# Mixing attention: two heads a step in the two halves of the TensorE array, and fewer key blocks for the neighbourhood heads

## The reference, cut to what matters

```python
def neighbourhood_attention(q, k, v, kc, vc, rpb):
    ...
    w_start = np.clip(q_col - NA_KW // 2, 0, GRID_W - NA_KW)[..., None]
    valid = (k_col >= w_start) & (k_col < w_start + NA_KW)   # 16 of the 64 columns
    ...
        s_lat = einsum('bjqhd,bijshd->bhjqis', q_r, k_r) * scale + bias
        s_lat = where(valid, s_lat, NEG_INF)
        s_ctx = einsum('bjqhd,blhd->bhjql', q_r, kc) * scale
        p = softmax(concatenate([s_lat, s_ctx], axis=-1))
        return einsum(p_lat, v_r) + einsum(p_ctx, vc)

def window_gqa_attention(q, k, v, kc, vc, sink):
    # 128 queries see keys at most 128 away, the context, and a sink logit
```

## Time and profile before

| | |
|---|---|
| median of 3 runs | 4348.28 us (4348.02 to 4357.41) |
| profiled execution, its own time | 4366.82 us |
| its span | 4365.0 us |
| mean granted clock of TensorE | 0.926 of full speed |
| busy, share of the span | PE 89%, DVE 44%, ACT 28%, POOL 24% |

### The profile page before, as it was taken

How to read it: one execution, slowest core, us unless ns; L and a number is a source line. 1 busy time by engine, 2 the same in 40 slices (tenths; PEclk the granted TensorE clock), 3 DMA queues, 4 the chain that set the end, 5 groups by cost and what they waited for, 6 DMA issues and landing times.

```text
span 4365.0 us, 55857 instructions
## 1 busy us (share of the span) xinstructions
PE 3873.9 (89%) x21157; PEld 3208.4 (74%) x21157; DVE 1926.2 (44%) x2729; ACT 1200.5 (28%) x1742; POOL 1031.9 (24%) x419
## 2 busy tenths in 40 slices
PE   3999996898969999889999688979997899888998
PEld 2888885756748888768888575667886799578755
DVE  7555444155553432444353614653226644530134
ACT  2212121044322121222111212433223523311353
POOL 1332331200112322213332120013442233023301
PEclk9999997988979999989999798989997999788998
DMA  4333321100013322123332121012332122012201
GB/s 163 125 126 125 106 96 57 45 26 5 25 44 96 111 91 92 63 68 105 101 111 92 44 87 37 9 39 72 96 96 87 46 81 87 1 53 66 74 1 49
DMA packets 88275, 316.33 MB, mean 72 GB/s; under 512 B 10688, under 2 KB 11712, under 8 KB 87488
## 3 DMA queue, kind: packets, MB, share of 16 engines
q1 hardware_dynamic: 85056, 300.44, 21.3%
q10 hardware_dynamic: 3072, 13.90, 1.0%
HBM read 312.20 MB, written 2.10 MB: 72 GB/s over the span
## 4 chain that ended last, share of the span: by engine, by line
issue 74%; POOL 16%; PE 8%; POOLq 0%; DVE 0%; ACT 0%; ACTq 0%
POOL w_parts L460 16%; PE psum L1418 4%; PE psum L1736 1%; PE psum L1720 1%; PE psum L1759 1%; PE psum L1745 1%; PE psum L1724 0%; POOLq L459 0%; POOLq L464 0%; PE psum L1738 0%; DVE final L1346 0%; DVE final L1347 0%; DVE sq_sum L1272 0%; POOLq L460 0%; PE psum L1726 0%
## 5 line engine op out<-in xcount | busy, mean ns | idle before, releaser
L1418 PE MATMUL psum<-h_parts,w_parts 128*128 128x512 f32 (+2 forms) x11904 | 2137.8, 343 | 97.5 <-DVE h_parts L860 60.9
L1418 PEld LDWEIGHTS psum<-h_parts,w_parts 128*128 128x128 f32 x11904 | 1854.9, 193 | 381.3 <-issue 71.4
L460 POOL TENSOR_TENSOR w_parts<-w_raw,w_parts 128x1024 fp32r<-128x1024 f32 x415 | 1031.7, 2487 | 3315.4 <-ACT w_parts L482 3315.4
L482 ACT ACTIVATE w_parts<-w_raw 128x1024 fp32r<-128x1024 f32 x415 | 439.0, 1060 | 2234.8 <-PE psum L1418 2001.4
L1418 PE MATMUL psum<-hidden_parts,w_parts 128*128 128x512 f32 x3696 | 681.9, 347 | 0.8 <-DVE hidden_parts L860 0.8
L1418 PEld LDWEIGHTS psum<-hidden_parts,w_parts 128*128 128x128 f32 x3696 | 584.1, 188 | 96.6 <-DVE hidden_parts L860 1.3
L964 DVE TENSOR_TENSOR to_split<-silu_gate,psum 128x768 f32<-128x768 f32 (+1 forms) x88 | 78.2, 888 | 779.6 <-PE psum L1418 779.6
L929 DVE SCALAR_TENSOR_TENSOR mod_ring<-mod_ring,cond_rows 128x1024 f32<-128x1024 f32 x128 | 254.3, 1987 | 0.0
L860 DVE TENSOR_TENSOR hidden_parts<-to_split,hidden_parts 128x768 f32 (+1 forms) x88 | 185.4, 2107 | 100.9 <-ACT hidden_parts L487 100.9
L1430 PE MATMUL psum<-w_parts,h_parts 128*128 128x256 f32 x1296 | 175.7, 303 | 53.5 <-POOL w_parts L460 53.5
L1430 PEld LDWEIGHTS psum<-w_parts,h_parts 128*128 128x128 f32 x1296 | 174.0, 212 | 55.5 <-issue 55.5
(11 more groups left out here) (265 smaller groups left out, 2821.4 us busy)
## 6 DMA issues: line engine op xcount, KB each, us to landing
w_raw<-wu_dram SPq DMA_DIRECT2D x415, 512.0 KB, 3.5
mod_ring<-modw_dram SPq DMA_DIRECT2D x128, 512.0 KB, 4.2
mod_first<-modw_dram SPq DMA_DIRECT2D x16, 512.0 KB, 5.1
na_bias<-rpb_dram ACTq DMA_DIRECT2D x24, 224.0 KB, 3.7
four_dft<-four_dram ACTq DMA_DIRECT2D x2, 2048.0 KB, 7.9
resid<-xT_dram SPq DMA_DIRECT2D x1, 2048.0 KB, 12.8
out_dram<-final SPq DMA_DIRECT2D x8, 256.0 KB, 2.0
cond_rows<-condb_dram SPq DMA_DIRECT2D x1, 1024.0 KB, 4.8
```

The costliest lines, as they stand in the source:

```text
L460: pool.tensor_tensor(SPL[:, s % 2, 1], RAW[:, s % 2], SPL[:, s % 2, 0].bitcast(F32), ALU.subtract).then_inc(w_split, 1)
L482: act.activation(SPL[:, u % 2, 0], RAW[:, u % 2], ACT.Copy).then_inc(w_hi, 1)
L1418: ins = pe.matmul(PS[:, pair, PSO[a]:PSO[a] + z - a], SPL[:, s, wp, k], src[:, xp, k, t0 + a:t0 + z], start=k == 0 and n_ == 0, stop=k == ...
```

## The change

`att_steps` now gives one step per pair of heads and query tile: 36 steps in layer 0, 24 in layer 1. The two heads stand in partitions 0 to 63 and 64 to 127. Scores of head x use rows 64x to 64x+63 of the array and go to PSUM banks x (latent) and 2+x (context); values of head x go to the partitions 64x to 64x+63 of bank 7, and the two heads alternate.

For the neighbourhood heads, queries, keys and values are stored column block by column block (16 columns of all 8 rows are a tile of 128, `NA_C`, `by_column`, `column_tiles`), so that a query tile needs only the key tiles that its columns can see (`NA_KEYS`): two for the outer tiles, three for the inner ones. The bias tensor is prepared for these tiles in the host's layout and loaded for two heads at once; the masks come in a tensor of their own. To store the neighbourhood values so, their three units (10 to 12) are now computed like the others with features on the partitions, copied by DVE in column order, and turned by PE transposes; unit 13 is a token unit alone, 14 and 15 stay a pair.

`scores` and the transposed probabilities change their buffers: two of `scores` (each for two heads), one of `probs_t` for both heads. DVE, ACT and PE work on both heads of a step: one instruction for both where the shapes allow it (bias, maximum, reciprocal, context copy), two where not (exponential, normalisation).

```diff
+NA_KEYS = [(0, 1), (0, 1, 2), (1, 2, 3), (2, 3)]
...
-    SB = place("scores", [P, 3, T1 + 8], F32, a_y + 8192)
-    PT = place("probs_t", [P, 2, T1], F32, a_y + 8192 + 3 * (T1 + 8) * 4)
+    SB = place("scores", [P, 2, 2, 648], F32, a_y)
+    PT = place("probs_t", [P, 2, 640], F32, a_y + 10368)
...
@@ ACT, iteration i @@
+                        if i >= 1:
+                            act.wait_ge(s_tr, tr0 + steps[i]["tr0"])
+                        act.activation(SB[:, a % 2, :, 1 + w:1 + w + CTX], row2(PSF[:, 2 * SEQ:4 * SEQ])[:, :, 0:CTX], ACT.Copy,
...
+                        for x in range(2):
+                            ins = act.activation(SB[:, a % 2, x, lo:1 + w], SB[:, a % 2, x, lo:1 + w], ACT.Exp,
+                                                 bias=SM[:, a % 2, 1, x:x + 1], accum_out=SM[:, a % 2, 2, x:x + 1])
...
+                        if i >= 2:
+                            act.wait_ge(s_pv, a)
+                        for x in range(2):
+                            act.wait_ge(s_tr, tr0 + st["tr0"] + x + 1)
+                            act.activation(PT[:, x, 0:min(w, SEQ)], bank(4 + x, min(w, SEQ)), ACT.Copy).then_inc(s_trc, 1)
+                        if st["tr"] == 3:
+                            act.wait_ge(s_tr, tr0 + st["tr0"] + 3)
+                            act.activation(PT[:, :, SEQ:SEQ + P], row2(bank(6, 2 * P)), ACT.Copy).then_inc(s_trc, 1)
...
@@ PE @@
-                for j in range(10, 16, 2):
-                    pe.wait_ge(psum_read, pr + j - 2)
-                    token_units(u + j, ...)
+                for j in range(10, 13):
+                    unit(u, 0, j, H, T1, DT, [(psum_read, pr + j - 3)])
+                    if j > 10:
+                        value_rows(j - 1)
+                pe.wait_ge(psum_read, pr + 10)
+                tiles = [(t * P, t * P) for t in range(6)]
+                token_units(u + 13, H[:].rearrange("p a k t -> p (a k t)"), tiles, n=1)
+                value_rows(12)
+                pe.wait_ge(psum_read, pr + 12)
+                token_units(u + 14, H[:].rearrange("p a k t -> p (a k t)"), tiles[0:T // P])
...
+                    if i >= 1:
+                        pe.wait_ge(s_lat, 24 * mx + st["nlat"])
+                        pe.wait_ge(s_ctx, a)
...
+                        for x in range(2):
+                            rows = slice(x * HD, x * HD + HD)
+                            pe.matmul(bank(x, k1 - k0), QK[rows, st["q"], t:t + P], QK[rows, st["k"], k0:k1], start=True, stop=True)
...
+                    for y, tt in enumerate(st["tt"]):
+                        for x in range(2):
+                            ins = pe.matmul(PSF[x * HD:x * HD + HD, o:o + P], VT[:, tt, st["vcol"][x]:st["vcol"][x] + HD],
+                                            PT[:, x, y * P:y * P + P], start=y == 0, stop=y == nt - 1, skip_group_check=True)
...
                 scores(0)
-                scores(1)
                 for i in range(N + 1):
-                    if i + 2 < N:
-                        scores(i + 2)
-                    if i < N:
-                        ...
-                        for x in range(len(st["tt"])):
-                            ins = pe.transpose(...)
-                        ins.then_inc(s_tr, 1)
+                    if i + 1 < N:
+                        scores(i + 1)
                     if i >= 1:
                         values(i - 1)
+                    if i < N:
+                        transposes(i)
```

More of the change, by code:

```diff
@@ L1508, in scores @@
-                    pe.matmul(PS[:, a % 2, SEQ:T1], q, QK[st["rows"], st["k"], SEQ:T1], start=True, stop=True).then_inc(s_mm, 1)
+                        for x in range(2):
+                            rows = slice(x * HD, x * HD + HD)
+                            pe.matmul(bank(x, k1 - k0), QK[rows, st["q"], t:t + P], QK[rows, st["k"], k0:k1], start=True, stop=True)
+                    for x in range(2):
+                        rows = slice(x * HD, x * HD + HD)
+                        ins = pe.matmul(bank(2 + x, CTX), QK[rows, st["q"], t:t + P],
+                                        QK[rows, st["k"], SEQ:T1], start=True, stop=True)
@@ L1510, in values @@
                 def values(i):
                     st, a = steps[i], a0 + i
-                    if i == 0 or steps[i - 1]["last"]:
-                        pe.wait_ge(v_ready, e + st["ot"])
-                    pe.wait_ge(s_trc, a + 1)
-                    o = PS[st["rows"], 3, st["t"] * P:st["t"] * P + P]
-                    nt = len(st["tt"])
-                    for x, tt in enumerate(st["tt"]):
-                        ins = pe.matmul(o, VT[:, tt, st["vcol"]:st["vcol"] + HD], PT[:, a % 2, x * P:x * P + P],
-                                        start=x == 0, stop=x == nt - 1)
+                    if st["first"]:
+                        groups = sum(s["last"] for s in steps[:i])
+                        if groups > 0:
+                            pe.wait_ge(s_out, o0 + groups)
```

289 lines of the change are left out of this document (173 added, 116 removed).

## The result

| | median us | ratio to before, 95% interval |
|---|---|---|
| before | 4351.62 (4348.02 to 4357.41, 4 runs) | |
| after | 4378.94 (4361.16 to 4381.92, 4 runs) | 1.0058 [1.0033, 1.0082] |

The changed kernel is 27 us slower. The profiled execution of after was its fastest (4361.16 us), that of before slower than its median, and they differ by 31 us in stages that the change doesn't touch, most of them feed-forward; so I compare stretches, not spans.

A forecast was written before the change was run, and what follows sets the result against it. PE, busy 89% of the 4365.0 us span, was taken as the bound. Attention +112 us and projections -14 gave +98, so 4446 us; range 4300 to 4520, the forecast's own 4407 to 4487.

The forecast's parts named there:

- The new wait: Mixing attention: PE and ACT take turns where they overlapped; PE stands still 3.1 to 3.6 us every step.
- The projections: Value and Fourier projections, both layers: -14 us together, between -18 and -8.
- rival 1: Attention: the clock stays up; attention -28, projections -14, total 4306 us, faster; chance 17%.
- 8.0 us each: Projections: PE time of each of three value units now computed in the common form, weights hidden.
- The wait: Projections: one 3.7 us wait before the last unit pair; before, three waits for POOL's low parts.
- the unit alone: Projections: one token unit in 144 instructions of 128 columns, 17 us, between 15.4 and 19.0.
- I take 80% of the attention's PE work at the lower level.: Attention: share of PE work slowed by the clock; -28 + 0.8 x 175 = +112 us.
- each such pause is enough to lose the clock, and the 6 to 8 us of work between two pauses seldom enough to get it back.: Attention: the reason given for the 80%, drawn from pauses of 3.19 and 4.67 us in before.
- my sum: Attention of both layers: 188 and 240 us at full clock, 267 and 337 at half, weighted 80% toward half.
- a mean of 7.2: Attention: full-clock step time in us, from 6.5 (4 blocks) and 7.9 (5 blocks).
- the three wide passes: Attention scores with 5 blocks: three wide passes in a row, making 1.67 us, against 1.35 for 4 blocks.
- Rival 1's point of decision: Attention: with less than about 24% of PE work at the lower level the change gains.

The follow-up runs named there:

- ten fillers: Changed kernel with ten extra matmuls of constants on PE between scores(i+1) and values(i-1) in each turn; 4292.58 us, ratio 0.9869.
- three fillers: Changed kernel with three extra matmuls of constants on PE in each turn, between scores(i+1) and values(i-1); 4310.39 us, ratio 0.9875.
- exponentials-first kernel: Changed kernel with ACT doing the exponentials of step i before the context copy of step i+1; 4286.59 us, ratio 0.9855.
- before in the new order: Kernel before with the changed kernel's PE order: scores(i+1), values(i-1), transposes(i); 4727.44 us, ratio 1.0845.
- the run by head: Changed kernel with the first head's block scores, context scores and value passes written before the second's, instead of alternating; 4424.57 us, ratio 1.0149.

## Why the prediction was right in sign and wrong in size

**Right.** The new wait, as told: scores release ACT, ACT's last copy releases PE, pauses of 3.07 to 3.56 us (forecast 3.1 to 3.6; only in layer 0's context steps they are shorter, 2.31 to 2.65), shown by the rows above and by the run that shortens what ACT does in them. The projections: -15.1 against -14, one POOL wait in place of three. The clock as the thing that decides: without its fall the attention is 407.0 us, which with the projections makes a faster kernel, as rival 1 had it.

**Right in part by luck.** In the sum for the projections "8.0 us each" was a slip: 80.05 us for 444 instructions are 8.65 for a unit's 48, and the trace after has 8.71. Three units make that some 2 us a layer too little. The wait (3.06 us for 3.7), the unit alone (16.28 for 17) and the transposes (2.0 for 2.4) came out below their terms by nearly as much, so the total held. No row shows the 107 ns that the 17 was partly set from: transposes of before start 0.11 us apart (2736.97, 2737.08, 2737.19), and the unit's 144 instructions ran at 113 ns each.

**Wrong: "I take 80% of the attention's PE work at the lower level."** It was 57%. The step before it failed: "each such pause is enough to lose the clock, and the 6 to 8 us of work between two pauses seldom enough to get it back." I had read a few single pauses as a rule for each turn, and took the one stretch in which the clock hadn't returned in 8 us (PE was in fact busy at 0.50 there for 18.7 us, from 2681.30 to 2700.00) for the usual case. In layer 1's loop, one pause in four of that length cost nothing, and after the others the clock was back within 3.3 to 5.9 us of work.

The attention came out at 492.3 us against 568 by my sum. The 76 us split so:

- Share at the lower level: (0.80 - 0.57) x 176 = 40 us. This is the step that failed.
- Full-clock turns: 407.0 us with the clock kept against my 428, so 21 us. A turn of 4 or 5 blocks takes 6.7 to 7.0 us; I had a mean of 7.2. The scores are the main part: 1.14 us for 4 blocks against 1.35, and 1.35 for 5 (2706.64 to 2707.99 with ten fillers) against 1.67, since I let the three wide passes stand in a row.
- Price of the lower level: 85.3 us for 57% of the work, where my turns give 0.57 x 176 = 100, so 15 us. There is less PE work to slow down, 184 us against the 210 in my shares.

Rival 1's point of decision (24% at the lower level) can be held against the runs: three fillers, with 21% and 11%, came out faster than before; after, with 57%, slower. The exponentials-first kernel, at 37%, lies above that point and is faster, but its round trip is shorter as well.

**Left open.** What besides the length of a pause decides whether the clock falls. Within after, the pause of 3.38 us costs nothing where the one of 3.07 does. In layer 1, pauses of 1.7 to 2.6 us went with a share of 0.36 (exponentials first), pauses of 1.7 to 2.2 us with 0.59 (before in the new order), and pauses of 2.2 to 2.7 us with 0.11 (three fillers). The changed kernel with PE's order of before (transposes ahead of values, scores two steps ahead, for which it would need more buffers) wasn't run. Layer 0's pauses in before weren't filled; at layer 1's gain it would be worth some 20 us, an estimate.

## What to carry to other kernels

When two engines come to wait for each other every turn, look first for an instruction in the shared engine's queue that doesn't need the new arrival and move it ahead: here one swap on ACT was worth some 90 us. Then price the pauses by the clock, in a range, and not by the worst stretch seen in another pattern; if they can't be removed, try a few matmuls into a spare piece of PSUM. Here ten a turn (2.50 us in pauses of 3.1 to 3.6 us) brought the share at the lower level from 0.62 and 0.51 to 0.02, and the turn stayed at 6.7 to 7.0 us; in the kernel with exponentials first, ten left no pause and made the attention 15.9 us longer than five. Compare a new scheme with the old one only when both have had this done.

## What the runs showed of the hardware that I had not expected

- Fillers of 0.75 us in a pause of 3.1 to 3.6 us cut the share at the lower level from 0.51 to 0.11 in layer 1 (0.62 to 0.21 in layer 0); fillers of 2.5 us to 0.02.
- In a loop with pauses of 3.1 to 3.6 us the clock came back after 3.3 to 5.9 us of fp32 work (layer 1), where in before PE was once busy at 0.50 for 18.7 us (2681.30 to 2700.00).
- Scores in row halves take 1.13 to 1.14 us for eight instructions of 256 columns whether the halves alternate or not, and matmuls of the second half start before earlier-written ones of the first (the rows of the run by head); values in column halves take 2.40 us for 20 when they alternate and 3.73 us when they don't, at the lower level.
